# Five matmuls per weight tile instead of six, with the token columns split 282 to 238, in a two-layer hybrid decoder step

## The chip, the cores and the metric

One core of a Trainium2 chip runs the whole program in one launch. The metric is the device time of an execution in microseconds, lower is better. Three runs of the kernel before stand below, and one more execution was taken with the hardware profiler.

## What is computed

A decoder trunk of two layers handles 512 prompt tokens and 8 sample tokens at once, TOK = 520 columns in all. Every layer is macaron style: half an FFN, a mixer, half an FFN, each behind an RMS norm. Layer 0 mixes with attention (FoX) and a gated delta net, layer 1 with an eight-head retention.

```python
def swiglu(x, w_gu, w_down):
    a, b = jnp.split(x @ w_gu, 2, axis=-1)
    return (jax.nn.silu(a) * b) @ w_down

# per layer li; the same for the sample tokens xs
xp = xp + 0.5 * swiglu(rmsnorm(xp, g_ffa), ffn_w_gu[li, 0], ffn_w_down[li, 0])
xp = xp + mixer(rmsnorm(xp, g_mix))
xp = xp + 0.5 * swiglu(rmsnorm(xp, g_ffb), ffn_w_gu[li, 1], ffn_w_down[li, 1])

# retention, after u @ w_in has been split into q, k, v, gate
q = rope(q, pos);  k = rope(k, pos) * RET_DK ** -0.5
inner = (q k^T * dmat) v;  cross = (q * decay) S;  S_new = S * decay^C + k^T v
y = (silu(gate) * head_layernorm(o) * gnorm) @ w_out
```

D_MODEL is 1024 (KD = 8 chunks of 128), D_FF 2816 (KF = 22 chunks), and w_in of the retention has 48 column blocks of 128 (six for a head: q, k, two of v, two of the gate).

## The kernel before

All activations lie transposed, features on the 128 partitions and the 520 tokens as columns. Products keep fp32 accuracy by two parts in the type fp32r: an activation is a high part (XH, HH, MOH, RMOH) and a low part (XL, HL, MOL, RMOL), a weight tile is WHI and WLO, and a product is high x high + low activation x WHI + high activation x WLO.

A **unit** is one load of weights: 8 chunks of 128x128, or 11 in the `down` stages. SP loads it into RAW (`load_unit`, L553), POOL splits it into WHI and WLO (`split_unit`, L713 and L716), TensorE multiplies it (`project`, L794), and `used` frees the buffer. Two such buffers alternate. In `project` each chunk takes six matmuls at L807: three products, each for two halves of 260 columns, into the two banks of an accumulator ACC[0..3] ([128, 2, 512] each). A **tile** is a finished accumulator; `tile_free` counts those that were read out.

The stages follow each other in program order: `up0`, `down0`, `ab_in`, attention and delta net, `ab_out`, `up1`, `down1`, `up2`, `down2`, `ret_in`, `ret_out`, `up3`, `down3`. Every engine has its own program of them.

- **up** (44 units of 8 chunks, accumulators 0 to 3 in turn): VectorE multiplies each tile by RSTD (L1815, L1818), ScalarE applies silu (L1416), VectorE multiplies both (TH, L1822), ScalarE makes HH (L1418), VectorE makes HL (L1824).
- **down**, `ab_out`, `ret_out`: an accumulator gathers two units (one in `ab_out`). VectorE adds it to X (L1799, in `update`), ScalarE squares X and makes XH (L1388, L1389), VectorE adds the squares (L1782) and makes XL (L1784). The first unit of the next stage waits chunk by chunk for XL (`xl_ready`).
- **ret_in** goes in turns, written out by hand (`ret_turn`, L1270 on TensorE, L2201 on VectorE). Turn h projects q, k and v of head h and, after these, the two gate tiles of head h-1, and between the projections the attention work of head h-1 is done. Two accumulators alternate, ACC[n % 2]. On TensorE the order in a full turn is: tile 0, transposes (L1284) and scores (L1308), tile 1, `kv` (L1317), tile 2, `o` (L1327, L1329) and `cross` (L1334), tile 3, `read` (L1343, L1345, L1347) and `mean` (L1351), tile 4, `var` (L1356), tile 5, `outer` (L1292). On VectorE: `scaled(0)` (L2209), the rotation into QB (L2213, L2218, L2221), `kd` and `att` (L2268, L2269), `scaled(1)`, the first rotation step of KB, the states `s0` to `s3` (L2285, L2290), the rest of KB, `scaled(2)`, `osum` (L2297), `scaled(3)`, `ov`, `os` and `osums` (L2304 to L2308), the centring (L2312), `sqsum` (L2315), `ga0` (L2241), the reciprocal (L2318), norm and gate (L2321, L2251), the low part (L2257), `ga1`, four state updates (L2235), gate and low part again. `kv` on TensorE waits for `att`, `o` for `s3`, `mean` for `osums`; the reciprocal waits for the root that ScalarE takes of `var`.

A `hold(engine, sem, value)` is a wait; `Steps.done` counts a named step on a semaphore and `await_step` waits for it.

## Time and profile before

| | us |
|---|---|
| runs | 2578.85, 2583.41, 2583.07 |
| median | 2583.07 |
| span of the profiled execution | 2571.9 |
| TensorE busy in it | 2477.0 (96%) |
| VectorE | 1270.5 (49%) |
| ScalarE | 565.3 (22%) |
| POOL (GpSimd) | 1680.7 (65%) |

The span goes from the first to the last instruction; the runs' times take in what lies around it. PE is TensorE's matmuls, PEld its weight loads, DVE VectorE, ACT ScalarE. Matmuls overlap in the records (one lasts longer than the step to the next), so steps between starts tell the rate, and busy shares don't.

### The profile page before, as it was taken

The numbers are of one execution on the slowest core, as the hardware profiler recorded it, in microseconds if no ns is written. First come the engines' busy times: TensorE is split into PE (matmuls) and PEld (weight loads), VectorE is DVE, ScalarE is ACT, GpSimd is POOL, SyncE is SP. The second block draws the span as 40 slices with busy tenths as digits, with TensorE's granted clock in tenths as the row PEclk, the third lists the DMA queues.
The fourth block names the chain that finished last, engine by engine and source line by source line (L and its number), as shares of the span: only waits on it lengthen the run. The fifth ranks groups of instructions, "written<-read, shape, count | busy, mean of one in ns | idle before, by whom it ended". The sixth has DMA issues, their size and how long they took to land.

```text
span 2571.9 us, 52956 instructions
## 1 busy us (share of the span) xinstructions
PE 2477.0 (96%) x20047; PEld 2384.1 (93%) x20047; DVE 1270.5 (49%) x2226; ACT 565.3 (22%) x848; POOL 1680.7 (65%) x750
## 2 busy tenths in 40 slices
PE   7999998998799899999999999999999899999997
PEld 7999998997577899999999999999999799999996
DVE  4444335787533654443344443367767644444433
ACT  3222101004733222220022220012222211222101
POOL 5777775664413477777777777765555367777773
PEclk9999999998899899999999999999999999999998
DMA  4333333895465333333323333233433333333331
GB/s 121 96 93 91 99 90 85 276 317 175 123 213 185 98 88 93 90 96 90 116 83 90 91 95 101 81 93 113 123 101 109 111 90 90 90 91 92 99 95 56
DMA packets 472391, 291.20 MB, mean 113 GB/s; under 512 B 32785, under 2 KB 438411, under 8 KB 472270
## 3 DMA queue, kind: packets, MB, share of 16 engines
q1 hardware_dynamic: 407286, 221.15, 29.6%
q10 hardware_dynamic: 64992, 68.54, 8.4%
q8 instruction: 72, 1.18, 0.2%
q14 instruction: 41, 0.34, 0.0%
HBM read 273.50 MB, written 16.23 MB: 113 GB/s over the span
## 4 chain that ended last, share of the span: by engine, by line
PE 86%; DVE 7%; ACT 3%; POOL 1%; issue 1%; ACTq 1%; DMA 0%; SPq 0%; DVEq 0%; POOLq 0%
PE ACC L807 76%; PE ACC L1075 2%; PE ACC L1044 1%; PE ACC L1317 1%; PE ACC L1327 1%; POOL WLO L716 1%; DVE TB L2318 1%; DVE RMOL L2257 0%; DVE XL L1784 0%; DVE SSR L2235 0%; PE ACC L1329 0%; PE ACC L1142 0%; POOL WHI L713 0%; ACT TAP L1497 0%; PE ACC L901 0%
## 5 line engine op out<-in xcount | busy, mean ns | idle before, releaser
L713 POOL TENSOR_TENSOR WHI<-RAW,ZERO 128x1024 fp32r<-128x1024 f32 (+1 forms) x341 | 691.5, 2028 | 665.0 <-PE ACC L807 625.8
L716 POOL TENSOR_TENSOR WLO<-RAW,WHI 128x1024 fp32r<-128x1024 f32 (+1 forms) x341 | 915.1, 2683 | 49.3 <-POOL WHI L713 2.3
L807 PE MATMUL ACC<-XH,WHI 128*128 128x260 f32 x4032 | 821.6, 285 | 4.2 <-DVE XL L1784 1.9
L807 PE MATMUL ACC<-XH,WLO 128*128 128x260 f32 x4032 | 812.8, 283 | 0.0
L807 PE MATMUL ACC<-XL,WHI 128*128 128x260 f32 x4032 | 811.1, 283 | 0.0
L807 PEld LDWEIGHTS ACC<-XH,WHI 128*128 128x128 f32 x4032 | 624.1, 189 | 22.9 <-DVE PRJ L1871 6.1
L807 PEld LDWEIGHTS ACC<-XH,WLO 128*128 128x128 f32 x4032 | 621.8, 189 | 0.0
L807 PEld LDWEIGHTS ACC<-XL,WHI 128*128 128x128 f32 x4032 | 620.5, 188 | 0.0
L807 PE MATMUL ACC<-HH,WHI 128*128 128x260 f32 x1408 | 284.1, 283 | 1.1 <-POOL WLO L716 1.1
L807 PE MATMUL ACC<-HH,WLO 128*128 128x260 f32 x1408 | 283.1, 282 | 0.0
L807 PE MATMUL ACC<-HL,WHI 128*128 128x260 f32 x1408 | 282.5, 282 | 0.0
L1818 DVE TENSOR_TENSOR TB<-ACC,RSTD 128x520 f32<-128x520 f32 x88 | 61.6, 700 | 420.8 <-PE ACC L807 420.8
L807 PEld LDWEIGHTS ACC<-HH,WHI 128*128 128x128 f32 x1408 | 216.8, 188 | 1.9 <-POOL WLO L716 1.9
L807 PEld LDWEIGHTS ACC<-HL,WHI 128*128 128x128 f32 x1408 | 217.2, 188 | 0.0
L807 PEld LDWEIGHTS ACC<-HH,WLO 128*128 128x128 f32 x1408 | 216.6, 188 | 0.0
L1824 DVE TENSOR_TENSOR HL<-TH,HH 128x520 f32 x88 | 163.5, 1858 | 88.4 <-ACT HH L1418 88.4
L1799 DVE SCALAR_TENSOR_TENSOR X<-ACC,X 128x520 f32 x48 | 33.6, 700 | 349.0 <-PE ACC L807 349.0
L1418 ACT ACTIVATE HH<-TH 128x520 f32 x88 | 56.4, 641 | 541.8 <-DVE TH L1822 541.8
L1822 DVE TENSOR_TENSOR TH<-TA,TB 128x520 f32<-128x520 f32 x88 | 155.2, 1764 | 8.5 <-ACT TA L1416 5.6
L1784 DVE SCALAR_TENSOR_TENSOR XL<-X,PAR,XH x48 | 157.9, 3289 | 0.5
L1388 ACT ACTIVATE SQ<-X 128x520 f32 x48 | 30.8, 641 | 579.3 <-DVE X L1799 579.3
L1416 ACT ACT_TABLE_LOAD x88 | 112.9, 1283 | 97.1 <-issue 95.9
(395 smaller groups left out, 2373.6 us busy)
## 6 DMA issues: line engine op xcount, KB each, us to landing
RAW<-in_ffn_w_gu SPq DMA_DIRECT2D x176, 512.0 KB, 3.8
RAW<-in_ffn_w_down SPq DMA_DIRECT2D x64, 704.0 KB, 4.7
KPAGES<-in_cache_fox_k ACTq DMA_DIRECT2D x128, 256.0 KB, 4.1
RAW<-in_c_w_in SPq DMA_DIRECT2D x48, 512.0 KB, 3.9
VPAGES<-in_cache_fox_v SPq DMA_DIRECT2D x72, 256.0 KB, 3.6
RAW<-in_ab_w_in SPq DMA_DIRECT2D x28, 512.0 KB, 5.7
VPAGES<-in_cache_fox_v ACTq DMA_DIRECT2D x56, 256.0 KB, 3.3
SSR<-in_state_ret_S ACTq DMA_DIRECT2D x8, 1024.0 KB, 6.6
```

Source lines behind the costliest of these rows:

```text
L713: pool.tensor_tensor(WHI[:, slot, 0:nk, :], RAW[:, slot, 0:nk, :], ZERO[:, :].broadcast_to([P, nk, P]), ALU.add).then_inc(hi_split, 1)
L716: pool.tensor_tensor(WLO[:, slot, 0:nk, :], RAW[:, slot, 0:nk, :], WHI[:, slot, 0:nk, :].bitcast(F32), ALU.subtract).then_inc(split, 1)
L807: ins = pe.matmul(ACC[acc][:, n, 0:HALF], w[:, slot, k, :], a[:, k0 + k, n * HALF:(n + 1) * HALF], start=first and opens, stop=final and c ...
L1075: ins = pe.matmul(bank(b)[:, h * P:(h + 1) * P], left(h), right(h), start=start, stop=stop)
L1388: act.activation(SQ[:, :], X[:, bass.ds(d, 1), :].rearrange("p a t -> p (a t)"), ACT.Square).then_inc(sq_ready, 1)
L1416: act.activation(TA[:, :], TA[:, :], ACT.Silu).then_inc(act_ready, 1)
L1418: act.activation(HH[:, bass.ds(j, 1), :].rearrange("p a t -> p (a t)"), TH[:, :], ACT.Copy).then_inc(hh_ready, 1)
L1784: dve.scalar_tensor_tensor(out=XL[:, bass.ds(d, 1), :].rearrange("p a t -> p (a t)"), in0=X[:, bass.ds(d, 1), :].rearrange("p a t -> p (a ...
L1799: dve.scalar_tensor_tensor(out=xd, in0=ACC[s][:, :, 0:HALF], scalar=scale, in1=xd, op0=ALU.mult, op1=ALU.add).then_inc(tile_free, 1)
L1818: dve.tensor_tensor(halves(TB[:, :]), ACC[2 * s + 1][:, :, 0:HALF], halves(RSTD[:, :]), ALU.mult).then_inc(tile_free, 1)
L1822: dve.tensor_tensor(TH[:, :], TA[:, :], TB[:, :], ALU.mult).then_inc(hfull_ready, 1)
L1824: dve.tensor_tensor(HL[:, bass.ds(2 * i + s, 1), :].rearrange("p a t -> p (a t)"), TH[:, :], HH[:, bass.ds(2 * i + s, 1), :].rearrange("p ...
```

## The change

In every projection but the attention's input (`project_ab` and the gate unit, which keep `project`), the 520 columns are parted at LEFT = 282 into left (282) and right (RIGHT = 238). The left part goes to the accumulator's first bank. The right part of the products with WHI is made by one matmul that reads both planes, high and low, of a now joint activation tensor (XS, HS, MOS, RMOS): its 476 columns land in the second bank as right (high) and right_low. So a chunk takes five matmuls. Whoever reads the accumulator now has to add the two right parts:

- in `update` VectorE does three operations for one, the last one waiting for the first (`right_added`);
- in `up` ScalarE copies right_low to LOWS (in SQ), and VectorE scales left, adds LOWS to right in the accumulator, and scales right. The waits are `lows_ready` and `lows_added`;
- in the retention VectorE alone scales right_low into RETLOW, scales right, scales left, and adds RETLOW to right (`scale_parts`, for `scaled` and `gate_tile`).

The joint tensors and RETLOW lie where the single ones and constants of layer 0 lay. The diff, cut to its core (calls that only pass XS for XH and XL, and the like, are left out):

```diff
+LEFT = 282
+RIGHT = TOK - LEFT
...
+        XS = new("XS", [P, 2, KD, TOK], F32R, "xs")
+        XH, XL = XS[:, 0], XS[:, 1]
...
+            def multiply(acc, slot, k, pair, chunk, opens, closes):
+
+                w_hi, w_lo = WHI[:, slot, k, :], WLO[:, slot, k, :]
+                out_right = ACC[acc][:, 1, 0:2 * RIGHT].rearrange("p (j t) -> p j t", j=2)
+                pe.matmul(left(acc), w_hi, pair[:, 0, chunk, 0:LEFT], start=opens, stop=False)
+                pe.matmul(out_right, w_hi, pair[:, :, chunk, LEFT:TOK], start=opens, stop=False)
+                pe.matmul(left(acc), w_hi, pair[:, 1, chunk, 0:LEFT], start=False, stop=False)
+                pe.matmul(left(acc), w_lo, pair[:, 0, chunk, 0:LEFT], start=False, stop=closes)
+                return pe.matmul(right(acc), w_lo, pair[:, 0, chunk, LEFT:TOK], start=False, stop=closes)
...
-                        project(u0 + 4 * i + s, (u0 + s) % 2, KD, s, XH, XL, ready=(xl_ready, KD * r + 1))
+                        project_by_parts(u0 + 4 * i + s, (u0 + s) % 2, KD, s, XS, ready=(xl_ready, KD * r + 1))
...
 (ScalarE, up)
+                def copy_lows(tile, acc):
+
+                    hold(act, used, u0 + tile + 3)
+                    hold(act, lows_added, 2 * KF * f + tile + 1)
+                    act.activation(LOWS[:, acc % 2, :], right_low(acc), ACT.Copy).then_inc(lows_ready, 1)
+
+                with act.Fori(0, KF // 2) as i:
+                    for s in range(2):
+                        copy_lows(4 * i + 2 * s, 2 * s)
+                        hold(act, tile_free, t0 + 4 * i + 2 * s + 5)
+                        act.activation(TA[:, :], TA[:, :], ACT.Silu).then_inc(act_ready, 1)
+                        copy_lows(4 * i + 2 * s + 1, 2 * s + 1)
+                        hold(act, hfull_ready, KF * f + 2 * i + s + 1)
+                        act.activation(HH[:, bass.ds(2 * i + s, 1), :].rearrange("p a t -> p (a t)"), TH[:, :], ACT.Copy).then_inc(hh_ready, 1)
...
 (VectorE, update)
-                        xd = X[:, bass.ds(d, 1), :].rearrange("p a (n t) -> p (a n) t", n=2)
-                        dve.scalar_tensor_tensor(out=xd, in0=ACC[s][:, :, 0:HALF], scalar=scale, in1=xd,
+                        xd = X[:, bass.ds(d, 1), :].rearrange("p a t -> p (a t)")
+                        dve.scalar_tensor_tensor(out=xd[:, LEFT:TOK], in0=right(s), scalar=scale, in1=xd[:, LEFT:TOK],
+                                                 op0=ALU.mult, op1=ALU.add).then_inc(right_added, 1)
+                        dve.scalar_tensor_tensor(out=xd[:, 0:LEFT], in0=left(s), scalar=scale, in1=xd[:, 0:LEFT],
+                                                 op0=ALU.mult, op1=ALU.add)
+                        hold(dve, right_added, KD * (r - 1) + d + 1)
+                        dve.scalar_tensor_tensor(out=xd[:, LEFT:TOK], in0=right_low(s), scalar=scale, in1=xd[:, LEFT:TOK],
                                                  op0=ALU.mult, op1=ALU.add).then_inc(tile_free, 1)
...
 (VectorE, up)
+                def scaled(out, tile, acc):
+
+                    hold(dve, used, u0 + tile + 3)
+                    dve.tensor_tensor(out[:, 0:LEFT], left(acc), RSTD[:, 0:LEFT], ALU.mult)
+                    hold(dve, lows_ready, 2 * KF * f + tile + 1)
+                    dve.tensor_tensor(right(acc), right(acc), LOWS[:, acc % 2, :], ALU.add).then_inc(lows_added, 1)
+                    hold(dve, lows_added, 2 * KF * f + tile + 3)
+                    dve.tensor_tensor(out[:, LEFT:TOK], right(acc), RSTD[:, LEFT:TOK], ALU.mult).then_inc(tile_free, 1)
...
 (VectorE, ret_turn)
+                def scale_parts(n, out):
+
+                    hold(dve, used, RU + first + n + 3)
+                    hold(dve, tile_free, RTILE + first + n + 4)
+                    dve.tensor_tensor(RETLOW[:, :], right_low(n % 2), RSTD[:, LEFT:TOK], ALU.mult)
+                    dve.tensor_tensor(out[:, LEFT:TOK], right(n % 2), RSTD[:, LEFT:TOK], ALU.mult).then_inc(ret_right, 1)
+                    dve.tensor_tensor(out[:, 0:LEFT], left(n % 2), RSTD[:, 0:LEFT], ALU.mult)
+                    hold(dve, ret_right, first + n + 1)
+                    return dve.tensor_tensor(out[:, LEFT:TOK], out[:, LEFT:TOK], RETLOW[:, :], ALU.add)
+
                 def scaled(n, out):
 
-                    hold(dve, used, RU + first + n + 3)
-                    dve.tensor_tensor(halves(out), ACC[n % 2][:, :, 0:HALF], halves(RSTD[:, :]), ALU.mult).then_inc(tile_free, 1)
+                    scale_parts(n, out).then_inc(tile_free, 1)
```

## Rows read from the trace of the kernel before

**Rows 1.** The page: span, TensorE's busy time and share, granted clock in 40 slices.

```profile
span 2571.9 us, 52956 instructions
PE 2477.0 (96%) x20047; PEld 2384.1 (93%) x20047; DVE 1270.5 (49%) x2226; ACT 565.3 (22%) x848; POOL 1680.7 (65%) x750
...
PEclk9999999998899899999999999999999999999998
```

**Rows 2.** The page: the chain that ended last, shares of the span by line.

```profile
PE ACC L807 76%; PE ACC L1075 2%; PE ACC L1044 1%; PE ACC L1317 1%; PE ACC L1327 1%; POOL WLO L716 1%; DVE TB L2318 1%; DVE RMOL L2257 0%; DVE XL L1784 0%; DVE SSR L2235 0%; PE ACC L1329 0%; PE ACC L1142 0%; POOL WHI L713 0%; ACT TAP L1497 0%; PE ACC L901 0%
```

**Rows 3.** Timelines of PE and of PEld in `up2`: start us, length us, instructions.

```profile
1500.08 0.40 PE L807 MATMUL ACC<-XH,WLO 128*128 128x260 f32 x2
1500.32 0.40 PE L807 MATMUL ACC<-XH,WHI 128*128 128x260 f32 x2
...
1500.20 0.30 PEld L807 LDWEIGHTS ACC<-XH,WHI 128*128 128x128 f32 x2
```

**Rows 4.** Busy time in a window of `up1`: PE, PEld, DVE, ACT, POOL, clock, DMA.

```profile
1000.00:1100.00 100.00, 100.00 (x835) 100.00 (x834) 42.23 (x35) 23.08 (x27) 77.34 (x35) 1.00 0.30 89
```

**Rows 5.** The chain through turns of the retention: start us, length us, what.

```profile
1812.60 0.44 PE ACC L1327 x4
...
1824.72 1.14 PE ACC L1351 x4
...
1831.59 0.88 PE ACC L1356 x4
1832.46 5.77 PE ACC L807 x48
...
1853.26 1.99 PE ACC L1317 x8
...
1873.14 1.15 PE ACC L1351 x4
```

**Rows 6.** Timeline of PE in `ab_out`, where the granted clock is half.

```profile
853.11 0.64 PE L807 MATMUL ACC<-MOL,WHI 128*128 128x260 f32 x2
853.54 0.64 PE L807 MATMUL ACC<-MOH,WLO 128*128 128x260 f32 x2
```

**Rows 7.** Timeline of PE: fp32 matmuls of 4 columns behind each other.

```profile
833.41 1.84 PE L1239 MATMUL ACC<-IDENT,VSUM 128*128 128x4 f32 x15
```

**Rows 8.** Another 4-column line: its durations in ns, least, median, most.

```profile
L1343 PE MATMUL ACC<-IDENT,READ x8: 170/252/253, 1822.5 to 1823.2; 128*128 128x4 f32 x8
```

**Rows 9.** Groups in the window 910 to 1150 (`up1`): busy us, mean ns | idle before, releaser.

```profile
L716 POOL TENSOR_TENSOR WLO<-RAW,WHI 128x1024 fp32r<-128x1024 f32 x42 | 106.5, 2537 | 7.2 <-POOL WHI L713 2.3 <-DMA RAW<-in_ffn_w_gu 0.4
...
L713 POOL TENSOR_TENSOR WHI<-RAW,ZERO 128x1024 fp32r<-128x1024 f32 x42 | 79.5, 1894 | 50.4 <-PE ACC L807 50.4
```

**Rows 10.** Timelines of PE at the start of `up2` and of `down1` [idle before, releaser].

```profile
1291.71 0.51 PE L807 MATMUL ACC<-XH,WHI 128*128 128x260 f32 x2 [0.38 <-DVE XL L1784]
...
1159.34 0.51 PE L807 MATMUL ACC<-HH,WHI 128*128 128x260 f32 x2 [0.27 <-POOL WLO L716]
```

**Rows 11.** Groups of DVE in the window 1671 to 2040 (`ret_in`), columns as rows 9.

```profile
L2285 DVE COPY SALL<-ACC 128x256 f32<-128x256 f32 x7 | 2.9, 412 | 0.0
...
L2304 DVE TENSOR_TENSOR WSC<-ACC,KVS 128x16 f32<-128x16 f32 x7 | 1.2, 175 | 2.2 <-PE ACC L1345 2.2
```

**Rows 12.** Timeline of DVE in two turns of the retention.

```profile
1810.65 1.51 DVE L2290 SCALAR_TENSOR_TENSOR SALL<-SALL,DECS,ACC 128x256 f32<-128x256 f32 x3
...
1833.23 3.40 DVE L2318 RECIPROCAL TB<-TB 128x520 f32<-128x520 f32 x1 [0.91 <-ACT TB L1749]
...
1852.53 0.68 DVE L2269 TENSOR_TENSOR TH<-ACC,DMAT 128x512 f32<-128x512 f32 x1
...
1853.72 1.86 DVE L2271 TENSOR_SCALAR QSD<-QB,DECS 128x8 f32<-128x8 f32 x1
```

**Rows 13.** Busy time in one stretch of `ret_in`, columns as rows 4.

```profile
1841.00:1888.00 47.00, 46.30 (x379) 43.97 (x378) 32.84 (x42) 13.34 (x21) 25.89 (x12) 1.00 0.38 115
```

**Rows 14.** Waits in the window 1671 to 2040: us in total, times, longest.

```profile
PEld ACC L1317 <- DVE TH L2269: 1.6, 6, 0.3
```

## What the change should do to the time

> **What bounds the kernel now.** I read the whole program first. TensorE is busy 96% of the span and its clock is full nearly everywhere [rows 1]; of the chain that ended last 76% is one line, the projection's matmuls at L807 [rows 2]. The busy share says nothing of the rate, so the second view is the timeline of one stretch: two matmuls of 260 columns start every 0.24 us, and this doesn't waver [rows 3]. A stretch of 100 us in an FFN layer counts 835 of them with those cut by its ends [rows 4], 120 ns each. Three products by two halves make six per weight tile of 128x128: 720 ns. Then the one place where another engine is as late as TensorE: the turns of the retention. There a turn takes 48.4 us (the `mean` matmuls of L1351 start at 1824.72 and 1873.14 [rows 5]).
>
> **What 120 ns consist of** decides the sign. 260 columns at 2.4 GHz are 108.3 ns. With the granted clock at half, the same matmuls go in pairs each 0.435 us [rows 6], 217 ns one, which is 260 columns at 1.2 GHz and nothing else. So at the full clock some 11.7 ns are on top of the columns. Where does this sit? Other rows bound it. Plain fp32 matmuls of 260 columns take 0.88 us for four [rows 5], 219 ns each; they take two cycles for a column, 216.7 ns, so their overhead is 2.5. Matmuls of only 4 columns, each with a weight load of 128, start each 0.113 us: fifteen in 1.84, the last one's 0.253 taken off, by 14 steps [rows 7, 8]: that is a floor of one load with one matmul, whatever the columns. Three readings fit:
> (a) a floor of about 120 ns for one load and matmul of this type, with a matmul over the floor costing columns plus 2.5;
> (b) 11.7 ns for every matmul;
> (c) slower columns, 0.452 ns each, plus 2.5.
> I take (a). The measured floor of 113 is the nearest row, 7 ns away, and above it no row shows more than 2.5 of overhead; (b) and (c) each need something that no fp32 row shows. The cold pairs don't decide it, as columns outlast everything there.
> The Trainium skill ("TensorE: Matmul & The Clock Gate", Back-to-back issue gap) gives N/2.4 + 2.5 ns at the full clock, and lets both load and matmul set the spacing of a stream. The trace has 120 where the formula gives 110.8. By the formula alone a tile would go from six times 110.8 to 662.5 ns, 2.5 saved; that speaks against this change and is the same saving as reading (c).
>
> **The change, part by part.**
> *Matmuls.* Per tile: left 282 columns three times, one matmul of 2x238 = 476, one of 238. The columns stay 1560, one load and one matmul of six go.
> (a): 282 columns need 117.5 + 2.5 = 120, thrice; 476 need 198.3 + 2.5 = 200.8; 238 need 101.7, so the floor, 120. Sum 680.8, saved 39.2 ns.
> (b): 3 x 129.2 + 210.0 + 112 = 709.6, saved 10.4.
> (c): saved 2.5.
> Converted tiles: four `up` of 44 units x 8 = 1408, four `down` of 16 x 11 = 704, `ab_out` 64, `ret_in` 384, `ret_out` 128. The attention's input projection keeps six. Outside `ret_in` these are 2304, nearly all where TensorE waits for nothing: 2304 x 39.2 = 90 us saved by (a), 24 by (b), 6 by (c).
> *Who must keep up.* A unit of `up` falls from 5.77 to 5.45 us. POOL needs 1.89 + 2.54 = 4.43 for its split, plus some 0.2 of waits [rows 9]: still under. SP issues the loads of weights a unit ahead, once POOL has split what lay in the buffer, in the order as before: nothing. In `up` VectorE is busy 42.2 and ScalarE 23.1 of 100 us [rows 4], 2.4 and 1.3 in a unit. Each scaling becomes three operations (about 0.55 more, priced below), ScalarE adds a copy of half a tile, at most the 0.6 or so that an operation on a whole one takes: 3.0 and 1.9 in 5.45. Each accumulator comes round after three other units, 16 us, which covers this. Were that cover gone, 0.55 us a unit on 176 units would be 97 us.
> *Borders of stages.* At the end of a `down` TensorE runs seven chunks of the next unit and then waits for the eighth: it waited for XL there, 0.38 us, and started at 1291.71 [rows 10]. The X update ahead of XL becomes three operations, +0.45, and the seven chunks are 0.27 shorter: +0.7, at five borders, 3.6 us. At the first unit of a `down` TensorE waits for the larger split (0.27 [rows 10]); +0.32 at four, 1.3. Together 5 us; nothing to 10 as bounds.
> *The retention's turns.* A scaling there is one VectorE operation of 0.69. It becomes four, all VectorE: by rows of 256 columns (0.412) and 16 (0.175) [rows 11] and 512 (0.68) [rows 12], 238 columns cost 0.40 and 282 cost 0.45, and operations in a row overlap by 0.07, so about 1.45 with an add at 0.40. Extra: 0.75. But the add has both inputs in SBUF, and such operations are stretched while POOL splits: one on 8 columns took 1.86 us beside it [rows 12]. So the extra is 0.75 to 2.4 us a unit; I take 1.1, since POOL is busy 25.9 of 47 us [rows 13], and where the next operation had been stretched by the same POOL split, part of this is taken back.
> Now the path. From `var` (1832.46) to `kv` (1853.26) TensorE has 20.8 us of work; VectorE has a closed chain there, from the reciprocal at 1833.23 through `ga1`, the state updates, `lo1`, the next head's first scaling and the rotation, to `att`, which ends at 1853.21, and TensorE waited on it six times, up to 0.3 us [rows 5, 12, 14]. VectorE has no air: two scalings, `ga1` and `scaled(0)`, lie in the chain, 2.2, and `ga0` pushes the reciprocal by 0.2: +2.4, and nothing of TensorE's gain in three units counts. From `kv` to `o` VectorE is 0.44 ahead (`s3` ends at 1812.16, `o` starts at 1812.60 [rows 5, 12]) and TensorE's unit shrinks by 0.3, so half of the scaling's 1.1 shows: about +0.4, as the rotation behind it takes back the rest. From `o` to `var`: two units save 0.63; `scaled(3)` precedes `ov` and delays `osums`, for which TensorE waits already, by 0.55: -0.1. A turn becomes about 51.1, +2.7. Seven full turns: +19; the first (four units, TensorE's) and the last take about +1. Sum +20, bounds +10 (extra 0.75) and +38 (every add blocked). What is late next: `att`.
> *Moves of RGATE, RETLOW, XS and the like* are addresses; nothing is issued for them. Each new wait on `ret_right` is for an operation with one operation after it; behind it are queued only the add and what follows in the same chain, already counted. In `up` VectorE waits on `lows_ready` for ScalarE's copy, about 0.1, within the cover.
>
> **The sum (a):** -90 + 5 + 20 = -65 us. The profiled execution's span is 2571.9 us, and the median of the runs is 2583.07, so 11.2 lie around the span and stay. 2571.9 - 65 + 11.2 = 2518.
> Its own range: with the 238-column matmul down at the 4-column floor (113) another 16 us go, and with the retention at +10, ten more: 2490. With the retention at +38 and the borders at 10: 2541.
>
> **Rivals.**
> 1. *Every matmul carries its overhead (b).* -24 + 4 at the borders; in a turn TensorE gains less, so +3.3 each, +23. About 2586. For it: each load starts at once with the matmul ahead of its own (load at 1500.20, its matmul at 1500.32 [rows 3]), as if it waited for that one and not the reverse. Against: the fp32 rows with 2.5.
> 2. *Slower: VectorE's chain in the retention on top of columns that set the rate (c).* Place: `var` to `att` in seven turns. Price: +3.5 a turn, +25 in all, and 3 at the borders, against 6 saved: 2605. It decides once a tile saves less than 12 ns (28/2304). For it: a VectorE chain with 0.3 us of room or less, and the same start of the loads as in rival 1. Against: the fp32 rows need no slower columns.
> 3. *The 476-column matmul doesn't stream:* it reads two planes, 238 columns of the high part and 238 of the low. No row has such an operand. A restart like a second matmul would take back the 39 but for the 2.5; then it is rival 2's time.
> 4. *The covers fail,* POOL or `tile_free` in the `up` stages, with (a): half of the gain, about 2555.
>
> **How the numbers follow.** (a) as summed 0.60, rival 1 0.14, rival 2 with 3 0.18, rival 4 0.08. The predicted time is (a)'s, 2518. The range goes from 2490 to 2590: it holds (a), 4 and 1, about 0.8; (a)'s own is 2490 to 2541. A measurement tells some 0.2% (5 us) from no change: faster 0.70 (a, 4, some of 1), same 0.11, slower 0.19.
>
> **What would show it.** In the `up` stages: five matmuls a tile, starts 120, 120 or 121, 201, 120 and 120 ns apart, so a unit of 5.45 us; if the 282s stand at 129 it is (b), at 130 with the 238 at 110 it is (c). In the retention: turns over 48.4 us, TensorE waiting for TH (`att`) before L1317 some 2 to 3 us a turn. POOL's split under a unit. Wrong would be: turns shorter than before; TensorE waiting in `up` for POOL or VectorE; a gain outside the retention under 60 us.

## The result: 2.8% slower, and the profile after

| | before | after |
|---|---|---|
| median of the runs, us | 2583.24 (2578.85 to 2586.48) | 2651.39 (2648.89 to 2657.78) |
| ratio, with its 95% interval | | 1.0279 [1.0262, 1.0295] |
| span of the profiled execution, us | 2571.9 | 2646.8 |
| TensorE busy, us | 2477.0 | 2506.6 |
| VectorE busy, us | 1270.5 | 1391.4 |

The ratio is estimated from the fast executions; the quotient of the two medians, 1.0264, lies inside its interval.

The page of the changed kernel, with the lines that answer to [rows 1] and [rows 2]:

```profile
span 2646.8 us, 49264 instructions
PE 2506.6 (95%) x17359; PEld 2333.2 (88%) x17359; DVE 1391.4 (53%) x2818; ACT 628.6 (24%) x1024; POOL 1670.1 (63%) x750
...
PEclk9999999998898999999999999998899899999998
...
PE 69%; DVE 9%; ACT 3%; issue 2%; POOL 1%; ACTq 1%; DMA 0%; DVEq 0%; POOLq 0%
PE ACC L818 16%; PE ACC L817 10%; PE ACC L819 10%; PE ACC L820 10%; PE ACC L821 8%; PE ACC L847 5%; PE ACC L1112 2%; DVE TB L2384 1%; PE ACC L1081 1%; DVE SSR L2303 1%; PE ACC L1321 1%; DVE VBH L2317 1%; PE ACC L1364 1%; PE ACC L1388 1%; PE ACC L1354 1%
```

Two things are to be seen. TensorE has 2,688 matmul records fewer and is busy 30 us *longer*. And the clock has fallen from 9 to 8 in the slices 28, 29 and 32, in which the retention runs.

**Where the time is.** I take the starts of GpSimd's splits as marks of the stages. Up to the first split of `ret_in` the kernel takes 1662.1 us against 1661.0; from there to the first split of `ret_out` 471.9 against 401.5; the rest 512.8 against 509.4. So +1.1, +70.4 and +3.4. The part that was to bring 90 us brings nothing, and the retention, which was to cost 20, costs 70. The kernel before was profiled in an execution some 9 us faster than its median, so the two spans differ by 75 us and the medians by 68.

**The rate of the five matmuls**, TensorE's timeline in `up1` (start us, length us, instruction), against [rows 3, 4]:

```profile
1000.02 0.30 PE L817 MATMUL ACC<-XS,WHI 128*128 128x282 f32 x1
1000.16 0.38 PE L818 MATMUL ACC<-XS,WHI 128*128 128x476 f32 x1
1000.38 0.29 PE L819 MATMUL ACC<-XS,WHI 128*128 128x282 f32 x1
1000.50 0.29 PE L820 MATMUL ACC<-XS,WLO 128*128 128x282 f32 x1
1000.63 0.28 PE L821 MATMUL ACC<-XS,WLO 128*128 128x238 f32 x1
1000.75 0.29 PE L817 MATMUL ACC<-XS,WHI 128*128 128x282 f32 x1
```

From L817 to the next L817 a tile takes 0.72 to 0.73 us, and there it had taken 720 ns with six matmuls. The mean steps in that window of 100 us are 132, 219, 128, 129 and 112 ns. The 282s (129 to 130 on average) and the 238 don't tell the prediction's readings (b) and (c) apart, which had them at 129 and 112, and at 130 and 110. The 476 columns do: 219, where (b) has 210.0 and (c) some 218. A unit of `up` takes 5.75 us (5.77 before), one of `down` 7.97 (7.93).

**The retention.** A full turn takes 58.0 us against 48.4. TensorE's waits in the window 1671 to 2110 (us in total, times, longest), which answer to [rows 14]:

```profile
PE ACC L1321 <- DVEq L2396: 27.6, 7, 9.0
PE ACC L1388 <- DVE SSQ L2374: 22.0, 7, 3.2
```

L1321 are the transposes, and L2396 is `states_stepped`, the signal behind the four state updates; L1388 is `mean`, L2374 is `osums`. For `att` (L1354), which was to be the late one, TensorE doesn't wait at all. Busy time in two stretches of a turn each (PE, PEld, DVE, ACT, POOL, clock, DMA), against [rows 13]:

```profile
1800.00:1856.00 56.00, 49.78 (x330) 45.77 (x329) 43.11 (x59) 13.31 (x21) 26.59 (x12) 0.91 0.32 97
1856.00:1912.00 56.00, 49.78 (x335) 45.84 (x335) 42.42 (x58) 11.37 (x20) 26.58 (x12) 0.93 0.32 97
```

Between the first `mean` and the last, 78.5 us ran at a granted clock of half (1.2 GHz); before it was 6.8. (An expectation below says 75.1; it leaves out one stretch of 3.4 us.) In a full turn the clock falls twice, each time while TensorE waits its 3 us, for 6.8 us around the wait for `osums` and 3.4 around that for the signal. The `mean` matmuls behind a wait (two in the kernel, four in the record):

```profile
1850.59 2.10 PE L1388 MATMUL ACC<-SSQ,ONES 128*128 128x260 f32 x4 [3.14 <-DVE SSQ L2374]
```

The same four `mean` matmuls took 1.14 us in [rows 5].

**The operation that waits.** VectorE's timeline in a turn, and then GpSimd's in the same stretch. L2273 is the fourth operation of a scaling, the only one of the four with both inputs in SBUF:

```profile
1803.13 1.21 DVE L2273 TENSOR_TENSOR RGATE<-RGATE,RETLOW 128x238 f32<-128x238 f32 x1
...
1815.39 0.39 DVE L2273 TENSOR_TENSOR RGATE<-RGATE,RETLOW 128x238 f32<-128x238 f32 x1
...
1829.52 1.21 DVE L2273 TENSOR_TENSOR TA<-TA,RETLOW 128x238 f32<-128x238 f32 x1
...
1839.41 1.59 DVE L2273 TENSOR_TENSOR VBH<-VBH,RETLOW 128x238 f32<-128x238 f32 x1
...
1848.62 1.92 DVE L2374 TENSOR_TENSOR SSQ<-VBH 128x8 f32<-128x8 f32 x1
```

```profile
1802.18 1.89 POOL L732 TENSOR_TENSOR WHI<-RAW,ZERO 128x1024 fp32r<-128x1024 f32 x1 [9.54 <-PE ACC L821]
...
1811.24 2.68 POOL L735 TENSOR_TENSOR WLO<-RAW,WHI 128x1024 fp32r<-128x1024 f32 x1
1815.85 1.89 POOL L732 TENSOR_TENSOR WHI<-RAW,ZERO 128x1024 fp32r<-128x1024 f32 x1 [1.93 <-PE ACC L821]
...
1828.57 1.89 POOL L732 TENSOR_TENSOR WHI<-RAW,ZERO 128x1024 fp32r<-128x1024 f32 x1 [8.32 <-PE ACC L821]
...
1838.09 2.65 POOL L735 TENSOR_TENSOR WLO<-RAW,WHI 128x1024 fp32r<-128x1024 f32 x1
...
1848.17 2.34 POOL L735 TENSOR_TENSOR WLO<-RAW,WHI 128x1024 fp32r<-128x1024 f32 x1
```

Put the ends beside each other. GpSimd's operation ends at 1804.07, the addition at 1804.34; 1830.46 and 1830.73; 1840.74 and 1841.00. Each time the addition ends 0.26 or 0.27 us behind GpSimd's. At 1815.39, with GpSimd idle since 1813.92, it takes 0.39. So it is throughout: of the 48 additions in the trace 32 started while a split ran, and all 32 end 0.26 to 0.27 us behind it; the other 16 take 0.39 or 0.40. Even the 8 columns of `osums` end with GpSimd's split (1850.54, 1850.51). This is what the Trainium skill ("SBUF — State Buffer", Who interferes with whom) states: a VectorE operation with two SBUF inputs shares a read interface with GpSimd's reads, and whoever comes second is blocked until the first has finished. The trace agrees. The 46 additions of the window 1671 to 2110 take 1.02 us on average (1.33 into VBH, 0.90 into TA, 0.81 into RGATE) where 0.39 is their own length.

They aren't the only ones. The gating, twice in a turn and also with both inputs in SBUF, is now the costliest group of VectorE in this window (count | busy us, mean ns). The changed kernel first, the kernel before second:

```profile
L2317 DVE TENSOR_TENSOR VBH<-RGATE,VBH 128x520 f32<-128x520 f32 x14 | 29.4, 2100 | 1.0
```

```profile
L2251 DVE TENSOR_TENSOR VBH<-RGATE,VBH 128x520 f32<-128x520 f32 x16 | 11.2, 697 | 1.2 <-DVE SSR L2235 0.2
```

It now takes 2.10 us in place of 0.70, though the change didn't touch it. In a full turn of the changed kernel it starts 0.45 us (the first) and 0.9 us (the second) behind the start of a split, and each ends 0.56 behind that split's end. In the kernel before it started some 0.3 or 0.7 us *ahead* of the next split, or with none near, and wasn't held up. So the longer scalings have moved it to the other side of a split's start. What a held operation has left when the split ends goes with its columns: 0.02 us for 8, 0.26 for 238, 0.56 for 520. Others got shorter; the first step of QB's rotation, 2.18 us in the kernel before and ending 0.56 behind a split there, takes 0.70.

### The profile page after: what moved, and what is told of

Its sections match the earlier page's. It is cut to its first block, busy times and chain, and to the rows that moved or that the text cites. A ratio compares the mean times of both kernels' runs of the same rounds, so it can differ in the third digit from the quotient of the medians.

```text
span 2646.8 us, 49264 instructions
## 1 busy us (share of the span) xinstructions
PE 2506.6 (95%) x17359; PEld 2333.2 (88%) x17359; DVE 1391.4 (53%) x2818; ACT 628.6 (24%) x1024; POOL 1670.1 (63%) x750
## 4 chain that ended last, share of the span: by engine, by line
PE 69%; DVE 9%; ACT 3%; issue 2%; POOL 1%; ACTq 1%; DMA 0%; DVEq 0%; POOLq 0%
PE ACC L818 16%; PE ACC L817 10%; PE ACC L819 10%; PE ACC L820 10%; PE ACC L821 8%; PE ACC L847 5%; PE ACC L1112 2%; DVE TB L2384 1%; PE ACC L1081 1%; DVE SSR L2303 1%; PE ACC L1321 1%; DVE VBH L2317 1%; PE ACC L1364 1%; PE ACC L1388 1%; PE ACC L1354 1%
## 5 line engine op out<-in xcount | busy, mean ns | idle before, releaser
L818 PE MATMUL ACC<-XS,WHI 128*128 128x476 f32 x1792 | 688.1, 384 | 0.0
L817 PE MATMUL ACC<-XS,WHI 128*128 128x282 f32 x1792 | 540.8, 302 | 6.5 <-DVE XS L1831 2.9
L820 PE MATMUL ACC<-XS,WLO 128*128 128x282 f32 x1792 | 524.7, 293 | 0.0
L819 PE MATMUL ACC<-XS,WHI 128*128 128x282 f32 x1792 | 523.9, 292 | 0.0
L821 PE MATMUL ACC<-XS,WLO 128*128 128x238 f32 x1792 | 494.6, 276 | 0.0
L820 PEld LDWEIGHTS ACC<-XS,WLO 128*128 128x128 f32 x1792 | 339.5, 189 | 52.8
L817 PEld LDWEIGHTS ACC<-XS,WHI 128*128 128x128 f32 x1792 | 344.5, 192 | 17.0 <-issue 7.9
L818 PEld LDWEIGHTS ACC<-XS,WHI 128*128 128x128 f32 x1792 | 344.2, 192 | 1.3
L819 PEld LDWEIGHTS ACC<-XS,WHI 128*128 128x128 f32 x1792 | 344.8, 192 | 0.0
L821 PEld LDWEIGHTS ACC<-XS,WLO 128*128 128x128 f32 x1792 | 341.6, 191 | 0.0
L818 PE MATMUL ACC<-HS,WHI 128*128 128x476 f32 x704 | 268.8, 382 | 0.0
L817 PE MATMUL ACC<-HS,WHI 128*128 128x282 f32 x704 | 207.3, 294 | 1.1 <-POOL WLO L735 1.1
L820 PE MATMUL ACC<-HS,WLO 128*128 128x282 f32 x704 | 205.8, 292 | 0.0
L819 PE MATMUL ACC<-HS,WHI 128*128 128x282 f32 x704 | 205.7, 292 | 0.0
L821 PE MATMUL ACC<-HS,WLO 128*128 128x238 f32 x704 | 193.8, 275 | 0.0
```

Source lines behind the costliest of these rows:

```text
L817: pe.matmul(left(acc), w_hi, pair[:, 0, chunk, 0:LEFT], start=opens, stop=False)
L818: pe.matmul(out_right, w_hi, pair[:, :, chunk, LEFT:TOK], start=opens, stop=False)
L819: pe.matmul(left(acc), w_hi, pair[:, 1, chunk, 0:LEFT], start=False, stop=False)
L820: pe.matmul(left(acc), w_lo, pair[:, 0, chunk, 0:LEFT], start=False, stop=closes)
L821: return pe.matmul(right(acc), w_lo, pair[:, 0, chunk, LEFT:TOK], start=False, stop=closes)
```

## The experiments

All edits are to the changed kernel but for that of e9, which is to the kernel before; the code cuts show the core of each. Ratios are to the kernel before on the same chip; its median there was 2577.78 us for e1, e2, e3 and e6, 2576.86 for e4, e5, e7 and e8, 2577.93 for e9 and e10, and 2575.40 for e11.

**Does anything outside the retention matter?**

```diff
 (TensorE, ret_turn)
-                    project_by_parts(RU + first + n, (RU + n) % 2, KD, n % 2, XS, ready=(xl_ready, KD * 4 + 1))
+                    project(RU + first + n, (RU + n) % 2, KD, n % 2, XH, XL, ready=(xl_ready, KD * 4 + 1))
 (VectorE, scale_parts: its four operations)
+                    return dve.tensor_tensor(halves(out), ACC[n % 2][:, :, 0:HALF], halves(RSTD[:, :]), ALU.mult)
```

> The retention's input projection goes back to six matmuls a tile and one scaling operation; all other stages keep five. Theory A (the loss of 68 us is VectorE's longer chain in the retention): the up stages already stand as before (a unit starts each 5.75 us in the changed kernel, 5.77 before), so the time is within 5 us of the kernel before, some 2587 us, ratio 1.000 to 1.003. Rival B (the regrouped matmuls and the extra VectorE and ScalarE work of the up and down stages carry a good part of the loss): over 2605, ratio over 1.008.

Measured: 2577.68 us, ratio 1.0003 [0.9993, 1.0014]. With the retention as before and five matmuls everywhere else, the kernel is where it was: a matmul less for each chunk of 128 rows, 2304 times, and the borders and added operations of `up` and `update` come to nothing together, within the 0.14% that the interval leaves. The whole loss is the retention's.

**Which half of the retention's change?** e2 has its five matmuls with the single scaling, e3 its four-part scaling with the six matmuls:

```diff
 (e2: VectorE)
-                    (the four operations of scale_parts)
+                    return dve.tensor_tensor(halves(out), ACC[n % 2][:, :, 0:HALF], halves(RSTD[:, :]), ALU.mult)
 (e3: TensorE)
-                    project_by_parts(RU + first + n, (RU + n) % 2, KD, n % 2, XS, ready=(xl_ready, KD * 4 + 1))
+                    project(RU + first + n, (RU + n) % 2, KD, n % 2, XH, XL, ready=(xl_ready, KD * 4 + 1))
```

> Five matmuls a tile in the retention too, but VectorE scales a tile in one operation on the first 260 columns of both banks; the right low part is left out and columns stand in the wrong place. Theory A: VectorE's chain is as long as before, so 2583 to 2590 us, turns of 48 to 49 us, and TensorE doesn't wait for the state updates. Rival C (the matmul over two planes is what costs in the retention, where the accumulators alternate by two): turns stay over 52 us, time over 2610.

> Six matmuls a tile in the retention, but VectorE does the four operations for each scaling, on whatever lies in those columns; the retention's output is then not the reference's. Theory A: the whole loss is there without the regrouped matmuls: 2640 to 2655 us, turns of 56 to 58 us, TensorE waiting 3 us or more a turn before the transposes for the state updates. Rival C: near 2590.

Measured: e2 2581.95 us, 1.0009 [0.9997, 1.002], a turn of 48.5 us. e3 2650.19 us, 1.0282 [1.0265, 1.03], a turn of 58.0. The loss is VectorE's three further operations per scaling, all of it. TensorE's waits in e3, the same two as in the changed kernel:

```profile
PE ACC L1388 <- DVE SSQ L2374: 22.0, 7, 3.2
PE ACC L1321 <- DVEq L2396: 18.7, 6, 3.2
```

**What does a column cost?** e6 puts a probe in the place of every projection of `up3`: for each chunk six equal matmuls into one accumulator, with another width per chunk.

```diff
-                        project_by_parts(u0 + 4 * i + s, (u0 + s) % 2, KD, s, XS, ready=(xl_ready, KD * r + 1))
+                        if f == 3:
+                            probe(u0 + 4 * i + s, (u0 + s) % 2, s, s, first)
+                        else:
+                            project_by_parts(u0 + 4 * i + s, (u0 + s) % 2, KD, s, XS, ready=(xl_ready, KD * r + 1))
```

> The last FFN layer's first product is replaced by a probe: each chunk has its own form of matmul, six in a row, each with its load of 128x128 weights: contiguous moving operands of 128 to 512 columns, operands over two planes (2x130 to 2x256), one form with only 32 weight columns, and plain fp32. The output is not the reference's. Column theory C (0.452 ns a column and 2.5): 512 columns start each 234 ns, 476 each 218, 400 each 183, 300 each 138, and two planes cost like one; 260 columns with 32 weight columns stay at 120. Overhead theory O (11.7 ns for every stretch of the moving operand): 512 each 225, 476 each 210 contiguous and 220 over two planes, 400 each 178, 300 each 137. Load theory L (the load of 128 weight columns costs the running matmul its 9 ns): as O but one plane or two alike, and with 32 weight columns 260 take 111 to 113. Under 250 columns all have a floor near 112.

Measured once (2739.0 us; the time means nothing here, the steps do). TensorE's timeline at its first unit. L908 reads one plane, L906 two; the first row holds six matmuls of 512 and six of 476 columns, the second six of 2x256 and six of 2x238:

```profile
2237.14 2.84 PE L908 MATMUL ACC<-XS,WHI 128*128 128x512 f32 x12
2239.82 2.86 PE L906 MATMUL ACC<-XS,WHI 128*128 128x512 f32 x12
2242.52 4.32 PE L908 MATMUL ACC<-XS,WHI 128*128 128x440 f32 x24
```

5928 columns in 2.68 us, from 2237.14 to 2239.82: 0.452 ns a column. The same in two planes takes 2.70. The mean steps between starts at the full clock, from the records of all eleven passes and without the first step of each chunk, which also depends on the width before it:

| columns | 128 | 200 | 238 | 250 | 260 | 282 | 320 | 400 | 476 | 512 |
|---|---|---|---|---|---|---|---|---|---|---|
| ns | 111.8 | 111.7 | 113.3 | 117.4 | 119.5 | 128.0 | 147.7 | 182.3 | 216.4 | 227.0 |

The floor is 112, not 120, and it ends at about 240 columns. Above it the columns set the step: 128.0 ns for 282 and 216.4 for 476 are 0.454 and 0.455 ns a column, and the formula of reading (c), 0.452 a column plus 2.5, comes within 2 ns of every width from 260 to 476. That is reading (c) for the widths of this change; (b) would have 210.0 at 476. At 512 the step is 0.443 a column, and (c), with 234, is 7 ns too high; the runs don't show why. By the sum of these steps the five matmuls need 128.0 x 3 + 217.7 (two planes of 238) + 113.3 = 715 ns and the six 717. The columns alone are 708 of both at 0.454. What the six carry on top is thus some 9 ns in all, and of the 7 that the five carry 5 are the 238's, which stands on the floor (its columns alone would be 108): 2 ns are left to save. Reading (a) had no such matmul, since its floor was under all the others too. With only 32 of the 128 weight columns loaded the steps are the same (119.8 for 260, 217.3 for 476), so the length of the load isn't what sets them. The Trainium skill ("TensorE: Matmul & The Clock Gate", Back-to-back issue gap) has N/2.4 + 2.5 ns as the gap of an isolated matmul; by that an estimate for 512 columns is 215.8. In this stream of loads and matmuls in fp32r it is 227.0, and the measurement decides. What the formula gives for the change, next to nothing saved, was right all the same.

**How does the length of a scaling come out?** e4 leaves the addition out, e7 keeps four operations but makes the addition in PSUM, with one input from SBUF:

```diff
 (e4)
-                    hold(dve, ret_right, first + n + 1)
-                    return dve.tensor_tensor(out[:, LEFT:TOK], out[:, LEFT:TOK], RETLOW[:, :], ALU.add)
 (e7: all four operations)
+                    dve.tensor_copy(RETLOW[:, :], right_low(n % 2)).then_inc(ret_right, 1)
+                    dve.tensor_tensor(out[:, 0:LEFT], left(n % 2), RSTD[:, 0:LEFT], ALU.mult)
+                    hold(dve, ret_right, 2 * (first + n) + 1)
+                    dve.tensor_tensor(right(n % 2), right(n % 2), RETLOW[:, :], ALU.add).then_inc(ret_right, 1)
+                    hold(dve, ret_right, 2 * (first + n) + 2)
+                    return dve.tensor_tensor(out[:, LEFT:TOK], right(n % 2), RSTD[:, LEFT:TOK], ALU.mult)
```

> The changed kernel with three operations per scaling in the retention in place of four: the last one, which adds RETLOW to the right columns with both inputs in SBUF, is left out, so the low part of 238 columns is missing from what is computed. In the changed kernel's trace these 46 additions took 1.02 us on average (0.39 where GpSimd had nothing under way, 1.2 to 1.6 where it had), the other three 0.40, 0.39 and 0.44. Theory (VectorE's chain in a turn is a closed loop, every us put into a scaling comes out once in each of the six scalings of a turn): the three that are left last some 1.1 us against 0.7 for the single one, 0.4 x 6 = 2.4 us a turn over 48.4, 51 us a turn, and 2578 + 7.2 x 2.4 = about 2595 us (2590 to 2605). Rival (what costs is that a scaling hands over in pieces, or the six-against-five matmuls on TensorE; the blocked addition lies beside a wait that is there anyway): turns of 55 to 58 us and 2635 to 2650.

> The changed kernel with as many operations per scaling, four, and the same result, but none of them with both inputs in SBUF: the low part is copied to RETLOW, added in PSUM to the right columns, and these are then scaled. The addition in PSUM took 0.41 us in the feed-forward parts of the changed kernel whatever GpSimd did (L1868, x17). Theory (the addition that waits for GpSimd's running operation is over half of what the scaling gained): a scaling takes 0.40 + 0.36 + 0.41 + 0.40 and some 0.1 us for the two waits, 1.6 to 1.7 us against 2.2 now and 0.7 before, so a turn of 54 us in place of 58, and 2578 + 7.2 x 5.6 = 2618 us (2605 to 2630). Rival (the number of operations is what counts, wherever they read): 58 us a turn and 2650; the two waits in a row could even make it 2655.

The edit of e4 also drops the count on `ret_right`, which nothing waits for then. Measured: e4 2586.04 us, 1.0037 [1.0023, 1.0051]; e7 2621.10, 1.017 [1.0143, 1.0196]. A scaling of e7 beside a split of GpSimd:

```profile
1849.47 0.41 DVE L2269 COPY RETLOW<-ACC 128x238 f32<-128x238 f32 x1 [3.08 <-PE ACC L821]
1849.79 0.44 DVE L2270 TENSOR_TENSOR RGATE<-ACC,RSTD 128x282 f32<-128x282 f32 x1
1850.15 0.40 DVE L2272 TENSOR_TENSOR ACC<-ACC,RETLOW 128x238 f32<-128x238 f32 x1
1850.59 0.41 DVE L2274 TENSOR_TENSOR RGATE<-ACC,RSTD 128x238 f32<-128x238 f32 x1
```

The addition into PSUM takes 0.40 us, and all 48 scalings of e7 last 1.51 to 1.53 us; those of the changed kernel last 1.38 to 2.60. Keeping the addition out of the way of GpSimd is thus worth some 29 us (2650.19 of e3, and 2651.39 of the changed kernel, against 2621.10), four operations or not. That isn't the length of the additions alone: in e7's turns the first gating, too, takes 0.70 where it took 2.39, `osums` 0.17 where it took 1.92, and less than half as much time is at half the clock. The series so far, with the time at half the clock between the first `mean` and the last:

| | scaling, us | turn, us | time, us | half clock, us |
|---|---|---|---|---|
| e2, one operation | 0.69 | 48.5 | 2582 | 11.0 |
| e4, three | 1.07 | 49.7 | 2586 | 10.2 |
| e7, four, none blocked | 1.52 | 54.7 | 2621 | 34.1 |
| changed kernel | 2.00 | 58.0 | 2651 | 78.5 |

The first 0.4 us cost 1.2 us a turn, half of what I had expected for six scalings in a closed chain (2.4), so there was some slack. The next 0.45 cost 5.0, nearly twice their sixfold, and the last 0.48 cost 3.3. In e4 TensorE waits in the steady turns for the states `s0` to `s3` (L2354), in e7 for `att` (L2336):

```profile
PE ACC L1364 <- DVE SALL L2354: 5.5, 6, 2.1
```

```profile
PE ACC L1354 <- DVE TH L2336: 25.2, 7, 4.0
```

The rows of e7's turn account for `att` at +25.6 us behind `var`, where it stood at +21.1. The second gate's scaling puts in 0.9; the second gating, L2318, takes 2.26 beside a split in place of 0.70, and its low part, L2324, 2.12 in place of 1.73; the next head's scaling puts in 0.8, and the rotation ends 0.8 later still, since its last step now takes 2.27 in place of 0.70 and its first 0.70 in place of 2.18. Why just these operations meet a split isn't shown. How an operation falls against the splits depends on the turn's length itself, which would make the time uneven in the scaling's length; this is argued, not shown.

**Is `states_stepped` the loop?** e5 moves the state updates and the signal ahead of the first gating and the second gate's tile; e8 does the same on top of e7.

```diff
+                    for n in range(STRIPS):
+                        state_update(n)
+                    await_step(dve, rm_dve, f"u{STRIPS - 1}", g)
+                    dve.sem_inc(states_stepped, 1)
                     await_step(dve, rm_dve, "n0", g)
                     gate(0)
                     gate_tile(1, 1 if is_last else 5)
-                    for n in range(STRIPS):
-                        state_update(n)
-                    await_step(dve, rm_dve, f"u{STRIPS - 1}", g)
-                    dve.sem_inc(states_stepped, 1)
                     gate(1)
```

> The changed kernel with VectorE's four state updates and the signal states_stepped moved ahead of the first gating and of the scaling of the second gate's tile; nothing is left out. In the changed kernel TensorE waited 27.6 us at 7 places for that signal before the transposes, none of it in the kernel before worth naming. Theory A (the loop runs over this wait): it goes to near zero, the transposes start some 3 us earlier in a turn (at 13.7 after the variance, as before), and 2 to 3 us of a turn come back: 2630 to 2637 us. Rival B (the wait is where the loop's length shows, not what sets it: the attention's own VectorE steps would be late next, since they stand behind the same operations in VectorE's queue): the wait moves to the scores' or the mean's, the turn changes by under 1 us, 2645 to 2655.

> Both edits together: the addition in PSUM and the state updates ahead of the gating; nothing is left out. If the scaling's length and the place of the updates are separate causes their gains add: by theory A and the blocked addition 2600 to 2615 us. By rival B the second edit adds nothing and the time is that of the addition in PSUM alone, about 2618. Neither is expected below the kernel before (2578), since the five matmuls gain TensorE under 1 us per tile in the retention (the column rate read from the width probe: 282 + 476 + 282 + 282 + 238 columns at 0.45 ns against six of 260).

Measured: e5 2647.56 us, 1.0281 [1.0253, 1.031], a turn of 57.9; e8 2605.95, 1.0117 [1.0093, 1.0142], a turn of 51.5. The waits of e5 for the signal (L2310 is its place there), and of e8 for its signal and for `att`:

```profile
PE ACC L1321 <- DVEq L2310: 21.3, 7, 7.2
```

```profile
PE ACC L1321 <- DVEq L2311: 12.9, 7, 6.9
PE ACC L1354 <- DVE TH L2336: 11.6, 7, 1.7
```

In e5 the signal is later than hoped. The transposes start 16.2 us behind `var`, 0.7 earlier than in the changed kernel, and VectorE's `att` stands at +24.9 in both. The 0.7 is worth 0.1 us a turn. So the wait on `states_stepped`, the longest of the changed kernel, is where the loop shows and not what sets its length: rival B. In e8 the same move is worth 15 us, and there the theory A of the expectation holds. The two aren't additive, which neither expectation said.

**What is the clock's share?** e10 lets TensorE work while it waits, on results that nobody reads:

```diff
+                    for _ in range(20):
+                        pe.matmul(ACC[1][:, 0, 0:P], ONES[:, :], IDENT[:, :], start=True, stop=True)
                     hold(pe, states_stepped, g + 1)
...
+                    await_step(pe, rm_act, "o1", g)
+                    for _ in range(24):
+                        pe.matmul(ACC[2][:, 0, 0:P], ONES[:, :], IDENT[:, :], start=True, stop=True)
                     await_step(pe, rm_dve, "osums", g)
```

> The changed kernel with TensorE kept at work in its two long waits of each turn of the retention: 20 multiplications of 128x128 by 128 columns (0.11 us each at full clock) into the free accumulator ACC[1] before it waits for states_stepped (3.1 us), and 24 into ACC[2] before it waits for osums (3.1 us). Their results are written over before anybody reads them; nothing else changes. In the changed kernel 75.1 us of the retention's turns ran at half the clock, in a stretch behind each of these waits. Theory A (half the clock is part of the loss, and what TensorE does in these stretches is on the path): the half-clock time falls below 20 us, and of the up to 5 us a turn that it costs most comes back: turns of 53 to 55 us, 2615 to 2630 us. Rival B (the chain on VectorE sets the turn and TensorE waits the longer at the next place): the clock recovers but turns stay within 1 us of 58, 2643 to 2655 us.

Measured: 2660.64 us, 1.0326 [1.0304, 1.0349], slower than the changed kernel. The half-clock time did fall, to 10.2 us, but the time lies in the range of neither theory. I had taken an instruction for a matmul; an fp32 matmul is two, 0.11 us each at 128 columns. TensorE's timeline of e10:

```profile
1910.40 5.52 PE L1390 MATMUL ACC<-IDENT,ONES 128*128 128x128 f32 x48
...
1936.39 4.73 PE L1341 MATMUL ACC<-IDENT,ONES 128*128 128x128 f32 x40
```

So they overran waits of 3.1 us by about 2. e11 has 10 and 12 in their place.

> As e10_keep_clock with half as many multiplications in each wait, 10 and 12: each of them is two passes of 0.11 us, so that the 20 and 24 took 4.7 and 5.5 us and overran the waits of 3.1 us that they were to fill by 1.6 and 2.1 us. Ten and twelve take 2.2 and 2.6 us and overrun nothing. Nothing else changes. In e10 the step from the mean to the variance, with one tile and four matmuls of the mean in it, fell from 9.3 us at half clock to 6.7, while the attention stood at 24.9 us after the variance as before: so the clock behind the mean's wait is on the path, that behind the transposes' wait is not. Theory A: transposes at 16.9, mean at 48.7, turn 58.0 - 2.6 = 55.4 us, and 2650 - 7 x 2.6 = 2632 us (2627 to 2638). Rival B: the turn stays at 57.5 or more and the time at 2643 to 2655; then the clock's 75 us beside the path cost nothing.

Measured: 2636.86 us, 1.0236 [1.0219, 1.0253], a turn of 55.7, half clock 6.8 us. A stretch of it, columns as above:

```profile
1800.00:1856.00 56.00, 53.77 (x389) 49.50 (x388) 44.10 (x59) 13.33 (x21) 26.83 (x12) 1.00 0.32 97
```

The clock is full in this stretch and 2.3 us of a turn come back, some 12 us in all (2646.8 to 2635.0 in the profiled executions): 22 needless matmuls a turn make the changed kernel faster. Theory A holds, and the time lies in its range. `att` stands at +24.9 still. What came back is the tile between `mean` and `var`: that stretch took 9.3 us in the changed kernel and 6.8 here. The half clock around the transposes' wait buys nothing: without it `kv` starts at +25.7 where it had been +26.4, but VectorE's `osums`, for which `mean` waits, ends no earlier, and `mean` stands at +48.9 against +48.7.

**Is there a version that beats both?** e9 makes the move of e5 in the kernel before (six matmuls, one scaling).

> The kernel before, with VectorE's four state updates and states_stepped moved ahead of the first gating and of the second gate's tile; nothing is left out. There TensorE's transposes waited at one place only (5.4 us, in the last turn), so the signal has no price in the steady turns: 48.4 us a turn and 2577 to 2578 us. It could be faster by up to 5 us (the wait in the last turn) or slower by up to 3 us (the gate's tile is scaled 2.7 us later, and TensorE's next-but-one tile waits for that).

Measured: 2591.77 us, 1.0053 [1.0038, 1.0068], outside what I expected. TensorE's first wait:

```profile
PE ACC L1317 <- DVE TH L2269: 11.7, 7, 1.8
```

`att` comes 23.1 us behind `var` in place of 21.1, a turn takes 50.4. In the kernel before, the order with the states late is the better one. No version here beats the kernel before: e1 equals it, and e4, which leaves out the addition that any real version must make, is already 0.4% slower.

## Why the prediction was wrong

It said 2518 us and faster with a chance of 0.70; the time was 2651, beyond the range and on the other side.

- *The choice of (a), worth 90 us.* This is the step that failed first. It took the 120 ns between starts for a floor of one load with one matmul. e6 shows the floor at 112, reached only below 240 columns, and above it a step that grows with the columns, some 0.455 ns each. The saving measured is about 2 ns a tile in `up` (5.77 to 5.75 us a unit of eight), a loss of 4 in `down`: nothing over 2304 tiles, as e1 confirms. (c) was written down with its right price, 2.5 ns, and turned down because the fp32 rows show 2.5 ns of overhead. Those rows are of another type (219 ns for 260 columns); what a column costs in fp32r they can't show. The row of 113 ns pointed the other way as well: it was read as "7 ns away", but it took a second assumption, a higher floor for this type, to make 120 out of it. And (c)'s own sum let the 238 columns stand at 110, under that floor; with 113 there it saves nothing at all.
- *Borders, +5.* In the profiled executions everything outside the retention came to +4.5, with the matmuls' gain near zero; e1, within 0.1% of the kernel before, leaves room for up to 3.6 us, so the term was about right or a little high.
- *The extra length of a scaling, 1.1 us.* Measured 2.00 - 0.69 = 1.3. The range of 0.75 to 2.4 held it; the mechanism, an addition stretched by GpSimd, was right. For `scaled(3)`, ahead of `osums`, the sum took 0.55 in place of its own 1.1 without a reason; measured there it is 1.5.
- *The retention, +20, with 38 as its bound.* This is the second step that failed. Measured 70. The chain from `var` to `att` was to grow by 2.4 us a turn and grew by 3.8 (21.1 to 24.9). From `att` on the prediction left almost nothing, and the trace has 5.8 there: `mean` stands at +48.7 against 41.7, and `var` 9.3 behind it where it was 6.7. Three things were left out. The operations beside the scalings that wait on GpSimd: the two gatings of a turn, 2.39 and 2.00 us where each took 0.70 (QB's rotation gives 1.5 of that back), and `osums`, 1.92 us on 8 columns where it took 0.53, and 0.17 with GpSimd idle. The `states_stepped` signal, the longest wait of the changed kernel, though e5 shows that it costs little by itself. And the granted clock, 2.3 us a turn by e11. From the first `mean` to the last, six turns of 48.4 and one of 37.1 became six of 57 to 58 and one of 44.3: 64 us, with 7 more ahead of them.
- *What is late next: `att`.* Wrong for the changed kernel, right for e7, e8 and e9.
- *Rival 2* was the right case: (c) with VectorE's chain, from `ret_in`, and it "decides once a tile saves less than 12 ns". Its 2605 was too low by the same missing 45 us of the retention, so even the right mechanism was priced at a third of the loss. Rival 3, a restart between the two planes, fell: 217.7 ns for 2x238, 216.4 for 476. Rival 4 didn't come: in `up1` and `up2` TensorE waits 0.8 us in all, for XL at a start.
- *Span and median.* I took 11.2 us as lying around the span. The changed kernel's profiled execution has 2646.8 of 2648.89, 2.1 around it. The other 9 us were an execution below its median, not time around a span.

## What to carry to other kernels

Before a change that trades instructions for equal work, find out what the step between two matmuls consists of: several widths in one probe tell a floor from a rate, one width can't, and two may mislead: 282 and 512 alone would give 0.43 ns a column with 7 on top, and miss 476 by 5. In a loop where one engine's chain sets the turn, price what an added operation *waits for*, not its own length: here an addition of 0.39 us cost 1.02 on average because GpSimd was splitting weights, and the same addition with an input in PSUM cost 0.40. Price also what a longer chain moves beside the other engine: the gating, untouched, went from 0.70 to 2.10. And a wait that TensorE gains can cost twice, by itself and through the clock of what follows.

## What I had not expected of the hardware

- fp32r matmuls, each with its load, step at the full clock by some 0.455 ns a column from 282 to 476 columns (128.0 and 216.4), 227.0 at 512, and 112 ns as the least; a second plane in the operand costs about 1 ns.
- A VectorE addition with both inputs in SBUF that starts while GpSimd's split is running ends 0.26 to 0.27 us behind it, 1.2 to 1.6 us in place of 0.39 with 238 columns; with 520 columns the end is 0.56 behind, with 8 it is 0.02 to 0.03. One that starts ahead of the split isn't held up (the gating in the kernel before, 0.70).
- With waits of 3 us on TensorE, twice in a turn, the matmuls behind them ran at half the clock for a while; 22 idle matmuls in such waits gave some 12 us back.
